# A float32 layer on Trainium2 whose weight split runs four pieces ahead of TensorE instead of six

## What is computed

```python
# first block
h = rmsnorm(x, pre_mix_gain)
q_sb, k_sb, v_sb, q_dl, k_dl, v_dl = split(h @ w_in)         # 2048 -> 6144, 8 + 8 heads of 128
o = concat(head_rmsnorm(stick_breaking_attention(q_sb, k_sb, v_sb)),
           head_rmsnorm(dilated_attention(rope(q_dl), rope(k_dl), v_dl)))
x = x + rmsnorm(o @ w_out, post_mix_gain)
u = conv3(rmsnorm(x, pre_ffn_gain) @ w_up)                   # 2048 -> 11008
x = x + rmsnorm((gelu(u_gate) * u_val) @ w_down, post_ffn_gain)
# second block
z = rms_norm(x) @ w_in_2                                     # 2048 -> 4096: xr, gr, gu, gv
a = gelu(gr) * (rglru(conv4(xr), forward) + rglru(conv4(xr), backward))
b = gelu(gu) * (w_s @ layer_norm(gelu(gv)) + b_s)
x = x + concat(a, b) @ w_out_2
# peer: 8 heads each choose 16 of 16384 experts by two searches over 128 keys
x = x + peer(rms_norm(x), w_q, sub_keys, expert_u, expert_v)
return rms_norm(x)
```

## Time and profile before

| | |
|---|---|
| median of 3 runs | 3210.3 us (3209.51 to 3211.92) |
| profiled execution | 3212.8 us, span 3211.5 us |
| granted TensorE clock, mean | 0.984 |
| TensorE matmul busy | 3087.5 us, 96% |
| TensorE weight load busy | 2828.2 us, 88% |
| VectorE busy | 1954.4 us, 61% |
| ScalarE busy | 1563.7 us, 49% |
| GpSimd busy | 607.9 us, 19% |
| memory traffic | 559 MB, mean 174 GB/s, queues at 49% of 16 engines |
| landing of a weight tile after its issue | 4.7 us, median |

### The profile page before, as it was taken

How to read it: one execution, slowest core, us unless ns; L and a number is a source line. 1 busy time by engine, 2 the same in 40 slices (tenths; PEclk the granted TensorE clock), 3 DMA queues, 4 the chain that set the end, 5 groups by cost and what they waited for, 6 DMA issues and landing times.

```text
span 3211.5 us, 50594 instructions
## 1 busy us (share of the span) xinstructions
PE 3087.5 (96%) x21302; PEld 2828.2 (88%) x21302; DVE 1954.4 (61%) x2614; ACT 1563.7 (49%) x2227; POOL 607.9 (19%) x411
## 2 busy tenths in 40 slices
PE   7999889999999998999998999999999999999998
PEld 6988769999998886988898998889999888999886
DVE  5444456555554445655699996446776545776545
ACT  4577645555554444675444444444444443444444
POOL 0011101111110000331134336002226001224300
PEclk9999999999999999999999999999999999999999
DMA  6533344555555554445444445554444554444553
GB/s 239 182 120 132 119 182 158 184 184 184 184 184 211 196 197 177 164 150 193 157 160 156 160 170 180 187 187 168 171 171 171 188 192 171 172 171 171 196 186 142
DMA packets 79858, 559.36 MB, mean 174 GB/s; under 512 B 9360, under 2 KB 10640, under 8 KB 12688
## 3 DMA queue, kind: packets, MB, share of 16 engines
q1 hardware_dynamic: 79632, 556.12, 48.7%
HBM read 553.99 MB, written 2.10 MB: 173 GB/s over the span
## 4 chain that ended last, share of the span: by engine, by line
PE 80%; DVE 3%; ACT 2%; issue 1%; POOL 1%; POOLq 0%; ACTq 0%; DVEq 0%
PE ps L250 15%; PE ps L251 14%; PE ps L252 14%; PE ps L261 12%; PE ps L263 12%; PE ps L262 12%; PE ps L1093 1%; ACT hiR L225 1%; PE ps L693 0%; DVE loR L233 0%; DVE eq L1032 0%; ACT fo L382 0%; PE ps L291 0%; DVE x L1472 0%; DVE eq L1038 0%
## 5 line engine op out<-in xcount | busy, mean ns | idle before, releaser
L233 DVE TENSOR_TENSOR loR<-raw,hiR 128x1024 fp32r<-128x1024 f32 x907 | 1138.5, 1256 | 1178.7 <-ACT hiR L225 1177.1
L225 ACT CAST hiR<-raw 128x1024 fp32r<-128x1024 f32 x1026 | 1074.8, 1048 | 1427.0 <-PE ps L252 741.7
L250 PE MATMUL ps<-XAh,hiR 128*128 128x256 f32 x4192 | 1220.0, 291 | 12.5 <-DVE x L1472 5.5
L251 PE MATMUL ps<-XAl,hiR 128*128 128x256 f32 x4192 | 1191.4, 284 | 0.0
L252 PE MATMUL ps<-XAh,loR 128*128 128x256 f32 x4192 | 1191.0, 284 | 0.0
L250 PEld LDWEIGHTS ps<-XAh,hiR 128*128 128x128 f32 x4192 | 808.5, 193 | 17.6 <-DVE x L1472 6.8
L251 PEld LDWEIGHTS ps<-XAl,hiR 128*128 128x128 f32 x4192 | 809.0, 193 | 2.8 <-issue 1.9
L252 PEld LDWEIGHTS ps<-XAh,loR 128*128 128x128 f32 x4192 | 808.5, 193 | 0.0
L233 POOL TENSOR_TENSOR loR<-raw,hiR 128x1024 fp32r<-128x1024 f32 x119 | 297.3, 2499 | 1405.8 <-ACT hiR L225 1405.8
L261 PE MATMUL ps<-hiR,ah 128*128 128x512 f32 x1024 | 404.5, 395 | 4.8 <-DVE al L1124 4.8
L263 PE MATMUL ps<-hiR,al 128*128 128x512 f32 x1024 | 404.3, 395 | 0.0
(11 more groups left out here) (256 smaller groups left out, 3058.9 us busy)
## 6 DMA issues: line engine op xcount, KB each, us to landing
raw<-in_u_dram SPq DMA_DIRECT2D x128, 1024.0 KB, 4.7
raw<-in_v_dram SPq DMA_DIRECT2D x128, 1024.0 KB, 4.7
raw<-in_w_up_dram SPq DMA_DIRECT2D x86, 1024.0 KB, 4.7
raw<-in_w_down_dram SPq DMA_DIRECT2D x43, 1024.0 KB, 4.7
raw<-in_w_in_qk_dram SPq DMA_DIRECT2D x32, 1024.0 KB, 4.7
raw<-in_w_out_dram SPq DMA_DIRECT2D x32, 1024.0 KB, 4.7
raw<-in_w_in_dram SPq DMA_DIRECT2D x24, 1024.0 KB, 4.7
raw<-in_w_in_v_dram SPq DMA_DIRECT2D x16, 1024.0 KB, 4.8
```

What stands on the lines that cost most here:

```text
L225: e.copy(hiR[:, r:r + 2, :], raw[n % NR][:, q:q + 2, :]).then_inc(S("hi"), 1)
L233: e.tensor_tensor(loR[:, r:r + 2, :], raw[n % NR][:, q:q + 2, :], hiR[:, r:r + 2, :].bitcast(F32), ALU.subtract).then_inc(S("lo_pool" if p ...
L250: e.matmul(dst, wh, X.h[:, k, :], start=(k == 0), stop=False)
L251: e.matmul(dst, wh, X.l[:, k, :], start=False, stop=False)
```

## The change

LA, the number of pieces by which the splits run ahead of the step, is 4 instead of 6. In the opening, which is written out by hand, the split of pair 4 is taken out of ACT's and DVE's first norm, because with LA = 4 the loop behind it makes that pair. The ring of eight pieces, its condition, the raw buffers and all else stay.

```diff
-NR, NQ, LA = 3, 8, 6
+NR, NQ, LA = 3, 8, 4
...
         split_hi(e, 2)
         for q in range(4):
             act_norm_hi(e, 0, q)
-            if q == 1:
-                split_hi(e, 4)
         e.wait_ge(S("start_const"), 48)
...
             dve_norm_lo(e, 0, q)
-            if q in (1, 3):
-                split_lo(e, 2 * (q // 2 + 1))
+            if q == 1:
+                split_lo(e, 2)
```

## The result

The changed kernel took 3190.56 us (median of 4 runs, 3189.64 to 3190.6), the kernel before it on the same chip 3211.11 (4 runs, 3209.51 to 3212.27): a ratio of 0.9936, 95% interval 0.9918 to 0.9953. The forecast was 3201.7, with 3191.5 to 3212.5 as its range. So the direction was right, and the gain, 20.5 us, was more than twice the 8.6 expected; the time lies just under the range.

A forecast was written before the change was run, and what follows sets the result against it. PE was taken as the bound, so a different split depth could change only its waits. Gains of 7.4, 2.4 and 8.4 against losses of 8.1, 0.3, 0.5 and 0.7 gave -8.6: 3210.3 to 3201.7 us, range 3191.5 to 3212.5.

The forecast's parts named there:

- What bounds the kernel: Whole kernel: PE is busy 3087.5 of 3211.5 us, bandwidth is not in the way, only PE's waits can change.
- Attention: Seven heads: the chain to line 412 starts earlier, saving 6.1 us there and 1.3 at line 436; bounds 0 to 16.5 plus clock.
- I take 7.4: Attention: the gain entered in the sum, 7.4 us, since the second cast is seen in the chain.
- W_out: Around W_out: gain 2.4 us, 1.4 at the last QK copy and 1.0 at the first bank's evacuation; between 0 and 5.7.
- Ends of the v ranges: Two v range ends: DVE adds to x earlier, gaining 2.50 us of wait and 1.7 of clock each, 8.4 together.
- Mixer: Three mixer periods: low parts come later behind the gate chain, loss 2.7 us each, 8.1 in all; layer norm ahead 0.5.
- W_out2: Fourth mixer period, beside W_out2, where no pair is on POOL: loss 0.3 us, between 0 and 1.3.
- Choice and decode: Choice and first decode: qT's copy gains 1.0 us, the decode loses 1.7, so +0.7, between -3 and +6.
- the first decode ends some 3 us sooner: Choice: DVE starts the last head's search earlier, having no ring-held pair in front, so the decode ends some 3 us sooner.
- a rival of +5: Decode is dearer: POOL and DVE lock each other once more, both exponentials hold a needed cast; 3206.7 us, chance 0.12.
- the heads clear altogether: Attention rival: all waits at lines 412 and 436 go, 15.2 + 1.3 instead of 7.4; 3192.6 us, chance 0.10.
- Slower: Rival: nine waits for low parts each grow by two pieces, 2.87 us, 25.8 in all; 3216.9 us, chance 0.10.

The follow-up runs named there:

- E6: Changed kernel with four extra 128x64 copies (1.08 us) on ScalarE behind the copy of QK, in each of the last seven heads: 3199.5 us, ratio 0.9968.
- E1: Changed kernel with the old lead of six in attention and the first two steps of W_out, four everywhere else: 3212.04 us, ratio to before 1.0007.
- E10: A lead of five pieces everywhere, instead of the changed kernel's four: 3190.42 us, ratio 0.9941.
- E9: Lead of four only up to piece 39 of W_out, the old six in all later steps: 3184.18 us, ratio 0.9924.
- E2: Changed kernel with lead six in the mixer up to P_WO2 + 18 and from P_Q + 48 to U0 + 48: 3180.59 us, ratio 0.9913.
- E7: Changed kernel with the old lead of six from the start of the choice to U0 + 48: 3184.95 us, ratio 0.9921.
- E5: Changed kernel with two extra 128x64 copies (0.54 us) on ScalarE behind the copy of QK, in each of the last seven heads: 3194.73 us, ratio 0.9952.

## Why the prediction was off

*What bounds the kernel*: right. The work is unchanged, PE's waits decide, and no stage held by the ring shows a wait for low parts. W_up's +0.9 is the clock: in its first 2.0 us after the change (465.40 to 467.40) the granted clock is 0.51 with 11 matmuls, before (490.10 to 492.10) 1.00 with 20.

*Attention*: the step that failed is "I take 7.4", a sum of waits in which the clock behind them stands at nothing. The mechanism of the waits stands: the held cast goes from the chain's start, the second one stays, and line 412 went from 2.17 to 1.2 each (6.7 us; 6.1 on record). Three things made up the rest. First, the clock. The prediction wrote "16.5 plus clock" as the upper bound of this part and then put no clock into its sum, although it did so at the ends of v, and gave no reason. Four falls at 1.7 are 6.8; E6's heads price one at 1.56, and the heads of before, 33.4 with a fall on average and 31.5 without, at 1.9. Second, the smaller waits around it, at lines 436 and 446, were 2.6 in this stage, of which only line 436's 1.3 was counted. Third, the last QK copy gave 2.0 for 1.4. That is 6.7 + 2.6 + 2.0 + 6.8 = 18.1 of the 20.1; the other 2.0 isn't assigned. E1 shows that all of it hangs on the lead in this stage. E6 shows that the wait at line 412 can bring falls, but with two of them for 3.1 us; why the old order had four, or five in E1, stays open.

*W_out*: the same step failed. The wait for the first bank gave 0.8 (1.0 on record), a wait at line 458 gave 0.4, and the two falls that were left out 3.4. That is 4.6 for the 4.3 measured. In E1 the wait of 3.3 has its fall again; E10, with the old wait of 2.4 for the first bank, shows none behind it.

*Ends of the v ranges*: right in mechanism and size, -8.7 for -8.4, the clock included: the falls behind both waits are gone. E9, with the old lead there, has the 5.5 again.

*Mixer*: right in size, +7.2 for +8.1 + 0.5, and in kind, several waits instead of one; E2 gives it all back. The waits grew by 2.7 in the second and the third period, as worked out, and by 1.3 in the first. Of the several waits the one for POOL's pair is the last, as said (2.1 at most), but not the costliest; 2.17 is for a pair on DVE.

*W_out2*: -0.2 for +0.3 is luck. Two waits of 0.80 and 1.48 for low parts came, 2.3 us and over the 0 to 1.3 on record. They don't show in the stage's length because its start (1457.60 to 1464.40) was at a granted clock of 0.50 before, and at 1.00 after (1441.00 to 1448.00). E2 has neither the waits nor the fall, and is 2.0 shorter (101.3).

*Choice and decode*: the direction was right, the term was mis-sized, +3.3 for +0.7. The copy of qT gave 0.9 (1.0 on record), and a wait at U0 + 22 came as named, at 6.49. The one named at U0+40 did not come, and the one at U0+34 stayed and grew to 4.13. The failed step here is "the first decode ends some 3 us sooner": it started 123.7 us into the choice instead of 122.1, while the stretching beside POOL rose from 10.2 to 20.1 us. In E7, where the order and the stretching are the old ones (10.1), it started at 121.5.
The rule for this is in the Trainium skill ("GPSIMD Engine Reference", 1. Specifications): GpSimd shares its SBUF interfaces with VectorE, with "contention with DVE instructions in a 2-port perf mode or with two SBUF inputs". The trace agrees on the second condition, line 1038 with two such inputs taking 4.48 beside a subtraction of POOL and 2.29 alone. A cast that reads one tile (line 1019) also took 2.04 beside POOL, in both kernels, and 0.22 alone, which that condition doesn't cover; whether it ran in the mode of the first one isn't seen in the trace. The prediction weighed a rule of this kind only at the ends of v, where the operand from PSUM kept clear of it, and priced this place as a rival of +5 with a chance of 0.12.

*Rivals*: "the heads clear altogether" came nearest in time, 3192.6, but for the wrong reason: the waits at line 412 did not clear, the clock did. "Slower" fell: the nine waits for low parts became eighteen and grew by 17.1 us in all, less than the 25.8 of two pieces each.

*The range*: it added up bounds of waits. The falls behind them, 10.2 us in six places, were outside it, and that is more than the 0.9 by which the time missed it.

## What to carry to other kernels

When a repeated wait is shortened, look at the granted clock of the stretch behind it, and put that into the sum with its own price and count: here it was worth as much as the wait. The count is the uncertain part and needs a range of its own, from none to one for each wait. A shorter lead in a shared instruction stream helps where a split held by a full ring stands ahead of something needed now, and hurts where the stage's own work is long; a lead for each stage took the gain without the loss. Where two engines that slow each other are both moved, price the overlaps anew, since an order that starts earlier can end later.

## What the hardware showed beyond the expected

Waits of 2.2 once a head (some 31 us) were followed by a stretch at the lower clock in three heads of before and the last, in five heads of E1, in two of E6, and in none where the wait was 1.7 (E5) or 1.2 (after), each counted in the one profiled execution. Runs with nearly the same idle time thus differed in the number of falls, and the mixer of E9 had none behind a wait of 3.3 that had one before, so that number can't be read from the waits alone. It may differ between executions of one kernel too: the 29 of the kernel before that were taken beside the experiments, on three chips, run from 3207.1 us, with a mean granted clock of 0.986, to 3215.5, with 0.983.

DVE and POOL delay each other in both directions: a DVE operation of 2.29 took 4.46 to 4.48 when POOL's subtraction had begun first, and POOL's operation of 1.26 took 2.18 when DVE's had. In both cases the delay is about what was left of the other's operation (POOL's ended at 1675.87, and 1675.87 + 2.29 = 1678.16 against an end at 1678.02; DVE's at 192.09, and 192.09 + 1.26 = 193.35 against 193.21).
